# One slot in four of a gated expert sum moved from the tensor engine to ScalarE and GpSimd

## The reference, cut to what matters

```
u    = expert_down[idx]                 # (tokens, heads, 16, 1024)
pre  = einsum('bthkd,btd->bthk', u, xb)
act  = gelu(pre) * gates
out  = einsum('bthk,bthkd->btd', act, expert_up[idx])
h    = h + out
```

## Time and profile before

| | before |
|---|---|
| median of 3 runs | 1624.59 us (1624.59 to 1627.25) |
| the profiled execution's own time | 1623.02 us |
| its span in the profile | 1621.3 us |
| mean granted TensorE clock | 0.957 of full speed |
| busy: PE, DVE, ACT, POOL | 1372.7, 1063.4, 390.5, 645.6 us |
| moved by the indirect gathers | 536.90 MB, 80.1% of 16 DMA engines' span |

### The profile page before, as it was taken

The page is one execution under the profiler, slowest core; times in us unless marked ns, Lnnn a source line. Parts: engine busy times, 40 slices in busy tenths (PEclk is TensorE's granted clock), DMA queues, the critical chain, the costliest instruction groups (busy, mean ns, idle before and its releaser), DMA issues.

```text
span 1621.3 us, 13943 instructions
## 1 busy us (share of the span) xinstructions
PE 1372.7 (85%) x4480; PEld 717.9 (44%) x4480; DVE 1063.4 (66%) x2712; ACT 390.5 (24%) x1038; POOL 645.6 (40%) x528
## 2 busy tenths in 40 slices
PE   8799999698888888888888898888888888888875
PEld 4357867444444444444444444344444444444332
DVE  2521577577676776767767667677676677776654
ACT  2012443122222222222222222222222222222221
POOL 0000000255445455445445454454455545544550
PEclk9989999899999999999999999999999989999999
DMA  5410520789999999999999999999999999999994
GB/s 158 123 52 27 219 110 2 288 344 420 421 408 420 422 421 421 389 422 422 421 421 420 420 417 391 422 421 420 422 416 422 420 384 422 422 420 421 422 421 199
DMA packets 84093, 568.85 MB, mean 351 GB/s; under 512 B 10003, under 2 KB 12596, under 8 KB 17460
## 3 DMA queue, kind: packets, MB, share of 16 engines
q0 software_dynamic: 73728, 536.90, 80.1%
q1 hardware_dynamic: 10292, 31.06, 5.8%
HBM read 564.26 MB, written 3.67 MB: 350 GB/s over the span
## 4 chain that ended last, share of the span: by engine, by line
PE 46%; DMA 27%; DVE 19%; ACT 4%; issue 3%; POOL 1%; SPq 0%; DVEq 0%; ACTq 0%; POOLq 0%
PE ps L907 25%; DMA arena<-in_experts_du_dram,arena 24%; DVE arena L649 10%; PE ps L788 6%; PE ps L739 4%; PE ps L771 4%; PE ps L743 2%; DMA line_scratch<-arena 2%; ACT arena L382 2%; ACT arena L262 1%; DVE arena L655 1%; ACT arena L377 1%; POOL arena L252 1%; DVE arena L557 1%; DVE arena L560 1%
## 5 line engine op out<-in xcount | busy, mean ns | idle before, releaser
L907 PE MATMUL ps<-arena 128*128 128x512 f32 x2048 | 960.2, 625 | 214.1 <-ACT arena L382 214.0
L252 POOL DMA_INDIRECT arena<-in_experts_du_dram,arena x512 | 643.7, 1257 | 943.1 <-PE ps L907 585.9
L649 DVE CUSTOM_DVE_ANT_0 arena<-arena 128x1024 f32<-128x1024 f32 x512 | 611.7, 1223 | 232.3 <-DMA arena<-in_experts_du_dram,arena 230.0
L907 PEld LDWEIGHTS ps<-arena 128*128 128x128 f32 x2048 | 397.2, 199 | 738.5 <-issue 462.7
L377 ACT ACTIVATE arena<-arena 128x4 f32<-128x4 f32 x128 | 26.3, 205 | 621.9 <-DVE arena L649 621.0
L382 ACT ACTIVATE arena<-ident,arena 128x128 f32<-128x128 f32 x512 | 163.6, 390 | 39.6 <-DVE arena L655 39.4
L262 ACT ACTIVATE arena<-ps 128x256 f32<-128x256 f32 (+1 forms) x114 | 51.9, 455 | 366.1 <-PE ps L788 336.9
L788 PEld LDWEIGHTS ps<-arena,wq 128*128 128x128 f32 x1024 | 119.2, 192 | 15.1 <-issue 14.3
L788 PE MATMUL ps<-arena,wq 128*128 128x128 f32 x1024 | 119.6, 275 | 0.5 <-ACT arena L262 0.5
L655 DVE SCALAR_TENSOR_TENSOR arena<-arena 128x4 f32<-128x4 f32 x128 | 28.4, 222 | 126.9 <-ACT arena L377 126.6
L739 PE MATMUL ps<-arena 128*128 128x512 f32 x208 | 96.4, 618 | 11.3 <-DVE arena L462 7.3
(11 more groups left out here) (152 smaller groups left out, 738.4 us busy)
## 6 DMA issues: line engine op xcount, KB each, us to landing
arena<-in_w_in_blocks_dram SPq DMA_DIRECT2D x18, 512.0 KB, 5.1
wq<-in_w_query_dram SPq DMA_DIRECT2D x1, 8192.0 KB, 33.7
arena<-in_experts_du_dram,arena POOLq DMA_INDIRECT x512
arena<-in_w_out_dram SPq DMA_DIRECT2D x1, 4096.0 KB, 14.1
h<-in_x_dram SPq DMA_DIRECT2D x4, 512.0 KB, 5.5
out_dram<-arena SPq DMA_DIRECT2D x4, 512.0 KB, 7.9
line_scratch<-arena SPq DMA_DIRECT2D x1, 1536.0 KB
arena<-line_scratch SPq DMA_DIRECT2D x1, 1024.0 KB, 5.9
```

Source lines behind the costliest of these rows:

```text
L252: gp.indirect_dma_start(rows[s % RING_E], None, experts_du, bass.IndirectOffsetOnAxis(ap=idx[:, (q // PH) % 2, q % PH * TOPK + i:q % PH * ...
L649: v.tensor_tensor_reduce(down, down, xn2[:, q // PH % 2, :], 1.0, 0.0, ALU.mult, ALU.add, pre[:, s % 16:s % 16 + 1]).then_inc(sem("dots"), 1)
L907: last = mm(ps[4 + 2 * (t % 2) + b][:], diag[:, s % 8, :], up[:, b * 512:(b + 1) * 512], start=False, stop=False, skip_group_check=True)
```

## The change

Of each group of four slots the first (s % 4 == 0) no longer goes through a diagonal and PE. ACT scales the up half of its row in place (128x1024) and raises `scaled`; POOL, in its own order and ahead of the gather that reuses the buffer, adds the up half to h in place (`add_row`, 128x1024) and waits for that add to complete. The three other slots go as before, counted by `pe_done`. Since h is now changed until the tile's last group, PE no longer starts the banks with identity times h but with slot 1 of the tile, and adds h at the tile's end (`add_mixed`), after waiting for the tile's 32 adds; `final_squares` waits for that. POOL's first add of a tile also waits until h has been read for the norm.

```diff
--- before.py
+++ after.py
@@ -40,6 +40,17 @@
 RING_E = 10
 NS = 4 * SLOTS
 NQ = 4 * PH
+ON_PE = GROUP - 1
+
+
+def by_pool(s):
+
+    return s % GROUP == 0
+
+
+def pe_done(s):
+
+    return s // GROUP * ON_PE + s % GROUP
 EPS = 1e-6
 NEG = -1e30
 LOWEST = -3.0e38
@@ -240,6 +251,15 @@
                 link(gp, gp.memset(xraw[:, j, 0:PAD], 0.0), "const", n)
             LOADS["const"] = n["const"]
 
+            def add_row(s):
+                t = s // SLOTS
+                gp.wait_ge(sem("scaled"), s // GROUP + 1)
+                if s % SLOTS == 0:
+                    gp.wait_ge(sem("h_mixed"), t + 1)
+                    gp.wait_ge(sem("xn2_ready"), t + 1)
+                up = rows[s % RING_E][:, D:2 * D]
+                link(gp, nc.gpsimd.tensor_tensor(h[:, t, :], h[:, t, :], up, ALU.add), "row_added", n)
+
             gp.wait_ge(sem("mixT_ps"), NT)
             for s in range(NS):
                 q, i = divmod(s, TOPK)
@@ -247,11 +267,16 @@
                     gp.wait_ge(sem("routed"), q + 1)
                 if s == 4:
                     gp.wait_ge(sem("wo_ps"), NT)
-                if s >= RING_E:
-                    gp.wait_ge(sem("row_free"), s - RING_E + 1)
+                if s >= RING_E and by_pool(s - RING_E):
+                    add_row(s - RING_E)
+                elif s >= RING_E:
+                    gp.wait_ge(sem("row_free"), pe_done(s - RING_E))
                 gp.indirect_dma_start(rows[s % RING_E], None, experts_du, bass.IndirectOffsetOnAxis(
                     ap=idx[:, (q // PH) % 2, q % PH * TOPK + i:q % PH * TOPK + i + 1], axis=0)
                     ).then_inc(sem(f"row{s % RING_E}"), 16)
+            for s in range(NS - RING_E, NS):
+                if by_pool(s):
+                    add_row(s)
 
 
         @block.scalar
@@ -377,9 +402,15 @@
                 nc.scalar.activation(gel[:, part], pre[:, part], ACT.Gelu).then_inc(sem("gelu"), 1)
                 act.wait_ge(sem("act_ready"), g + 1)
                 for s in range(GROUP * g, GROUP * g + GROUP):
-                    if s >= 8:
-                        act.wait_ge(sem("row_free"), s - 7)
-                    nc.scalar.activation(diag[:, s % 8, :], ident[:], ACT.Copy, scale=actv[:, s % 16:s % 16 + 1]
+                    if by_pool(s):
+                        up = rows[s % RING_E][:, D:2 * D]
+                        nc.scalar.activation(up, up, ACT.Copy, scale=actv[:, s % 16:s % 16 + 1]
+                                             ).then_inc(sem("scaled"), 1)
+                        continue
+                    d = pe_done(s) - 1
+                    if d >= 8:
+                        act.wait_ge(sem("row_free"), d - 7)
+                    nc.scalar.activation(diag[:, d % 8, :], ident[:], ACT.Copy, scale=actv[:, s % 16:s % 16 + 1]
                                          ).then_inc(sem("diag"), 1)
 
             def squared(t):
@@ -391,7 +422,7 @@
                 copy(xn2[:, t % 2, :], h[:, t, :], "sq_h", ACT.Square, accum_out=ss[:, 4 + t:5 + t])
 
             def final_squares(t):
-                act.wait_ge(sem("row_free"), SLOTS * (t + 1))
+                act.wait_ge(sem("acc_full"), t + 1)
                 final = xn2[:, t % 2, :]
                 copy(final[:, 0:512], ps[4 + 2 * (t % 2)][:], "fin_sq", ACT.Square, accum_out=ss[:, 12:13])
                 copy(final[:, 512:], ps[5 + 2 * (t % 2)][:], "fin_sq", ACT.Square, accum_out=ss[:, 13:14])
@@ -901,12 +932,20 @@
                 last.then_inc(sem("mixT_ps"), 1)
             def expert(s):
                 t = s // SLOTS
-                pe.wait_ge(sem("diag"), s + 1)
+                d = pe_done(s) - 1
+                pe.wait_ge(sem("diag"), d + 1)
                 up = rows[s % RING_E][:, D:2 * D]
                 for b in range(2):
-                    last = mm(ps[4 + 2 * (t % 2) + b][:], diag[:, s % 8, :], up[:, b * 512:(b + 1) * 512],
-                              start=False, stop=False, skip_group_check=True)
+                    last = mm(ps[4 + 2 * (t % 2) + b][:], diag[:, d % 8, :], up[:, b * 512:(b + 1) * 512],
+                              start=(s % SLOTS == 1), stop=False, skip_group_check=True)
                 last.then_inc(sem("row_free"), 1)
+
+            def add_mixed(t):
+                pe.wait_ge(sem("row_added"), SLOTS // GROUP * (t + 1))
+                for b in range(2):
+                    last = mm(ps[4 + 2 * (t % 2) + b][:], ident[:], h[:, t, b * 512:(b + 1) * 512], start=False,
+                              stop=True, skip_group_check=True)
+                last.then_inc(sem("acc_full"), 1)
 
             out_projection(NT - 1)
             pe.wait_ge(sem("wq_in"), 48)
@@ -920,12 +959,12 @@
                         pe.wait_ge(sem("final_ready"), t - 1)
                     elif t == 0:
                         pe.wait_ge(sem("h_mixed"), NT)
-                    for b in range(2):
-                        mm(ps[4 + 2 * (t % 2) + b][:], ident[:], h[:, t, b * 512:(b + 1) * 512], start=True,
-                           stop=False, skip_group_check=True)
                 for n_group in range(4):
                     for s in range(GROUP * (4 * q + n_group), GROUP * (4 * q + n_group + 1)):
-                        expert(s)
+                        if not by_pool(s):
+                            expert(s)
+                    if r == PH - 1 and n_group == 3:
+                        add_mixed(t)
                     if q + 3 < NQ:
                         if n_group == 0:
                             if r == 5:
```

## The result

| | before | after |
|---|---|---|
| median of the runs | 1625.76 us (4 runs, 1624.59 to 1627.25) | 1634.26 us (4 runs, 1632.07 to 1636.82) |
| profiled execution, its span | 1623.02, 1621.3 us | 1632.07, 1630.1 us |
| mean granted TensorE clock | 0.957 | 0.884 |
| last dot starts, and from there to the span's end | 1602.75, 18.55 us | 1609.01, 21.1 us |

The ratio is 1.0055, 95% interval 1.0038 to 1.0072: slower by 8.5 us on the medians, half a per cent, clear of the 0.2% that the prediction said could be told from no change. The forecast was 1627.4, with a range that reached to 1650 and a chance of 0.43 for slower. In the profiled execution the 8.8 us are 6.3 up to the last dot, so in the stream of gathers, and 2.5 behind it. A second profiled execution of the same kernel (first experiment, span 1630.4) has its last dot at 1610.79 and 19.6 us behind it: 8.0 and 1.1.

What follows compares the result with a forecast made beforehand. The prediction took the DMA gather stream at 421 GB/s as the bound. Start 0.4, boundaries 2.1 and tail 1.06 made 3.6, less half of up to 1.6: +2.8 on 1624.59 gave 1627.4 us, range 1619 to 1650.

Steps and rivals of the forecast that it cites:

- Rival A: Slower: POOL becomes the bound once add and wait together pass 3.43 us; +24 us, 1648 us, chance 0.25.
- C: A little slower: PE idles, groups begin at the lower clock, query comes late, tightest slots run dry; 1633 us, chance 0.15.
- The bound: Inside the tiles the DMA stream at about 421 GB/s bounds the kernel; 512 slots take 1275 us of 1621.3.
- Part 1: Work leaving PE, 1.78 us per group, 228 us in all, is worth nothing inside a tile, hidden by the DMA stream.
- Part 2: Group's new steps: scale 1.06 us, add 2.4; first buffer free at T + 3.7, 1.0 later; group 1 up to 0.7 earlier.
- Part 3: DVE and POOL exclude each other: an add waits up to one dot, 1.22 us, a dot up to 2.4 us.
- I cost the inside of the tiles at 0: Later buffer releases inside tiles cost nothing, hidden by the queue; without it each group would pay 1 to 2 us.
- a late release of 2.2 us: At worst, a full wait, a group's first buffer is 1.0 + 1.2 us later, against slack of 1.7 and 4.8.
- Behind group 0 little to meet: Behind group 0 DVE is in searches of one input, so POOL's add would hardly collide with it; no size given.
- Part 4: Start: first reissue 0.7 earlier, next dry spot 0.7 later, taken as +0.4; three tile boundaries 0.7 each, +2.1 in all.
- Part 5: The bare tail: PE again needs 7.13 us, but behind the scale, +1.06 us; the add is hidden.
- B: Faster: a shorter PE queue gives back the dry spots at the three tile boundaries, 9.6 us less 1.06; 1616 us, chance 0.10.

Runs made afterwards that it cites:

- first experiment: The changed kernel run again with no edit, as the anchor of the series: 1632.42 us, ratio 1.0047 to the kernel before.
- experiment 3: Kernel before with slot 0 of each group left out of the sum: no scale, no add, no product on PE; 1623.27 us, ratio 0.9986.
- experiment 5: Changed kernel, but PE adds the slot ACT scaled, as a product with the identity, and POOL adds nothing: 1647.16 us, ratio 1.0149.
- experiment 9: Kernel before with ACT scaling slot 0 but nobody adding it; its buffer is free when PE has finished slot 1: 1638.28 us, ratio 1.0080.
- experiment 4: Changed kernel with POOL's add replaced by two memsets that read nothing, scaled slot left out of the sum: 1626.93 us, ratio 1.0015.
- experiment 7: Changed kernel with each POOL add done twice, so one slot in four counts double in the sum: 1905.99 us, ratio 1.1741.
- Experiment 2: Changed kernel with PE also multiplying a block of zeros (4 records) at the end of each group but a tile's last: 1630.52 us, ratio 1.0034.

## Why the prediction was right and wrong

The chance was nearly even between same and slower, the likeliest figure +2.8 us, and it became +7.7 to +8.5. The forecast's own range, 1624 to 1631, was missed; that 1634.26 lies inside the range as a whole is luck, since its upper part stood there for rivals A and C, neither of which came about as described. Two terms put at zero were not zero, and the boundaries moved the other way.

- **The bound** held: DMA at 421 GB/s wherever the queue is full, in every run.
- **Part 1**, PE's relief at nothing inside a tile: measured 2.3 us of gain by itself (experiment 3, interval 0.5 to 4.2), and 9 us where the group starts late (5 against 9). The likely reason is that the tight gathers wait for PE (slots under 3 us of slack fall from 20 to 10 in the table); that is not shown apart.
- **Part 2**: the scale 1.15 us for 1.06, the add 2.36 undisturbed (median) and 2.44 on the mean for 2.4. The Trainium skill's figure (GPSIMD Engine Reference, section "Elementwise — side-by-side cycle accounting"), halved, gave an estimate of 2.25; the trace has 5% more. The first gather started 1.3 us later after T, for the 1.0 forecast, and took longer itself (1.65 us at 807.22 for 0.94 at 802.00). Group 1's T came 0.7 us earlier, as forecast.
- **Part 3** had the mechanism right: the row at 804.67 is a dot that waited 2.14 us, and experiment 4 took the cause away alone. **The step that failed is "I cost the inside of the tiles at 0".** It set a late release of 2.2 us against slacks of 1.7 and 4.8: by its own numbers the tightest gathers were not covered, and it trusted that DVE's free time would make up for it. It also counted one release at a time. The table shows that the round trip of a buffer grew by 1.4 us, as I read it because lateness of DVE, ACT and POOL adds up around the ring, and gathers with under 3 us of slack went from 20 to 54. At the group in which DVE norms the next tile the queue then ran dry, in two tiles (in one of them in the second execution): in the one shown above the gap between two gathers grew by 2.3 us against a slack of 2.9, with other small delays on top. These two places lie in the slices that lost 5.3 us. That term measured 4.7 us from experiment 3 to 4 (the scale and POOL's time) plus 5 from 4 to 1 (the exclusion), less the 2.3 of relief.
- Of the exclusion I had priced the dots only. A cast and the index product wait as well: 32 x 1.18 and 32 x 1.19 us for the two in the list above, on DVE's way to the next dots. "Behind group 0 little to meet" was wrong.
- **Part 4**: at the start the first reissue came at 324.11, 2.8 earlier; the gathers before it began 1.95 earlier too (299.82 for 301.77), so 0.85 earlier, 0.7 forecast. By the landing events the lead of 1.95 was used up by slot 24, which landed at 370.94 for 370.97, so the start cost more than the +0.4 forecast. The next dry spot's gather came at 337.23 for 339.31, level but for that shift, and took 1.7 us for 0.94, so it ended 0.65 later: 0.7 forecast. The boundaries did not get worse by these slices: their three slices lose 2.7, 2.5 and 2.1 us where before they lost 3.1, 2.9 and 3.6. +2.1 was forecast, -2.3 came.
- **Part 5**: +1.06 forecast; +1.1 in one profiled execution and +2.5 in the other. The second has PE at its low level (1.2 GHz) for part of the tail; these are its PE rows and the clock there:

```profile
1612.27 6.93 PE L939 MATMUL ps<-arena 128*128 128x512 f32 x12 [4.48 <-ACT arena L413]
...
1619.04 1.88 PE L946 MATMUL ps<-h,ident 128*128 128x512 f32 x4
```
```profile
1610.00:1614.00 4.00, 1.73 (x2) 0.84 (x3) 0.46 (x3) 2.23 (x5) 1.94 (x1) 0.74 0.00 0
1614.00:1618.00 4.00, 4.00 (x9) 1.81 (x8) 0.00 (x0) 0.00 (x0) 0.41 (x1) 0.83 0.00 0
```

PE needs 1620.92 - 1612.27 = 8.65 us for the 16 records of the earlier trace rows, 7.13 there.

- **Rival A** did not come about: add and wait together are 2.44 us, not 3.43. Its arithmetic holds roughly: experiment 7, where POOL had one more add per group, lost (1905.99 - 1632.42)/124 = 2.2 us per group. **B**: the boundaries gave back 2.3 of 9.6 us, and more was lost elsewhere. **C**: the clock did fall, to 0.884. Experiment 2 puts 2 us on it, unresolved, and experiment 3 has the low clock without a loss; its 1633 is near the measured time by luck, but tight slots ran dry as it says, mainly for other reasons.

Open: how the 4.7 us between experiments 3 and 4 divide between the scale and POOL's time (3, 4 and 9 differ in more than one wait), why experiment 9 is 11 us slower than 4, and what the clock is worth by itself. No run separated these.

## What to carry to other kernels

In a kernel bound by a stream through a ring of buffers, take stock of the ring: the mean time from landing to reissue, how many transfers have little slack, and above all the one group in a tile that is late already. Work moved off an engine that is hidden behind the stream still changes that time, both ways; three quarters of a microsecond on the step that everybody waits for cost more here (experiment 5: 0.76 us, 23 us of kernel) than a quarter of the largest busy group saved (experiment 3: 2.3 us). A two-input add on GpSimd beside a VectorE that runs two-input instructions costs both of them, also where the VectorE instruction is tiny.

## What the runs showed of the hardware that I had not expected

- Small VectorE instructions wait for a GpSimd add as the dots do, here on the mean of 32 each: a 128x32 cast 1365 ns for 181, an index product of 128x16 1362 for 175. Beside memsets of the same total length the product is back at 175 ns, the cast only at 666. The Trainium skill (SBUF — State Buffer, section "Who interferes with whom") lets casts enter a two-port mode that shuts GpSimd out altogether and two-input instructions only meet GpSimd reads; the trace agrees, with these numbers.
- A 128x16 subtraction with one tensor input and a per-partition scalar from SBUF (line 592) took 744 ns on the mean beside adds, 243 beside memsets, 234 before: it too waited for adds and not for memsets.
- Two adds of 512 columns, one behind the other, were 24 us worse for the kernel than one of 1024.
